# Block two with tokens on the partitions where the residual is added: 512-column weight streams instead of 256-column token streams

## The reference, cut to what matters

```
def hybrid_layer(x, ...):
    h = rmsnorm(x, norm_mix)             # x * rsqrt(mean(x*x) + 1e-6) * gain, per token
    z = h @ w_in                         # 1024 -> 4360 columns
    ... attention and mLSTM on z, two branch products, gates -> mixed
    x = x + mixed @ w_out                # 1024 x 1024
    u = jax.nn.relu(rmsnorm(x, norm_ffn) @ w_ff1)     # 1024 x 4096
    return x + (u * u) @ w_ff2           # 4096 x 1024
```

## Time and profile before

| | us |
|---|---|
| median of 3 runs | 2544.05 |
| lowest, highest | 2542.25, 2546.1 |
| the profiled execution's own time | 2542.61 |
| its span, first to last instruction | 2540.5 |

### The profile page before, as it was taken

How to read it: one execution, slowest core, us unless ns; L and a number is a source line. 1 busy time by engine, 2 the same in 40 slices (tenths; PEclk the granted TensorE clock), 3 DMA queues, 4 the chain that set the end, 5 groups by cost and what they waited for, 6 DMA issues and landing times.

```text
span 2540.5 us, 52442 instructions
## 1 busy us (share of the span) xinstructions
PE 2460.0 (97%) x20070; PEld 2318.3 (91%) x20086; DVE 1879.5 (74%) x2879; ACT 1278.6 (50%) x2103; POOL 1075.1 (42%) x620
## 2 busy tenths in 40 slices
PE   6999999999999999999999999999999999999999
PEld 4998999887989989989998788999889999989999
DVE  5875999678686787769997776775856677756676
ACT  3444456456554454444554565544654444654444
POOL 2434987412033233369872110333650344750344
PEclk9999999899999999999999999999999999999999
DMA  9885764333477568767643235875434466434564
GB/s 367 294 287 183 262 219 140 111 108 105 145 262 267 190 244 285 257 224 244 202 129 107 92 102 183 288 256 174 140 118 142 159 194 193 150 118 148 161 195 133
DMA packets 131496, 481.35 MB, mean 189 GB/s; under 512 B 14848, under 2 KB 14848, under 8 KB 130560
## 3 DMA queue, kind: packets, MB, share of 16 engines
q1 hardware_dynamic: 106992, 388.49, 45.8%
q0 software_dynamic: 23040, 83.90, 9.2%
q10 hardware_dynamic: 1296, 6.64, 0.7%
HBM read 475.82 MB, written 3.15 MB: 189 GB/s over the span
## 4 chain that ended last, share of the span: by engine, by line
PE 80%; DVE 9%; ACT 3%; POOL 3%; DVEq 2%; issue 1%; DMA 1%; ACTq 0%; SPq 0%; POOLq 0%
PE ps L473 23%; PE ps L474 22%; PE ps L475 22%; PE ps L627 2%; DVE ps L1754 2%; POOL eb L2147 1%; POOL ring_parts L2093 1%; ACT high L1143 1%; PE ps L1016 1%; PE ps L1005 1%; PE ps L484 1%; DVEq L1764 1%; DMA z<-ada_dram 1%; PE ps L487 1%; PE ps L485 1%
## 5 line engine op out<-in xcount | busy, mean ns | idle before, releaser
L474 PE MATMUL ps<-u_parts,high 128*128 128x256 f32 x3808 | 1061.8, 279 | 0.0
L474 PEld LDWEIGHTS ps<-u_parts,high 128*128 128x128 f32 x3808 | 720.2, 189 | 0.4
L1143 ACT ACTIVATE high<-ring 128x1024 fp32r<-128x1024 f32 x493 | 518.9, 1057 | 364.0 <-PE ps L475 329.4
L473 PE MATMUL ps<-ac_parts,high 128*128 128x256 f32 x1952 | 541.4, 277 | 9.9 <-DVE ring_parts L1541 9.4
L475 PE MATMUL ps<-ac_parts,ring_parts 128*128 128x256 f32 x1952 | 539.8, 277 | 0.0
L2098 POOL TENSOR_TENSOR ring_parts<-ring,high 128x1024 fp32r<-128x1024 f32 x88 | 223.5, 2539 | 407.9 <-ACT high L1143 407.8
L473 PE MATMUL ps<-h_parts,high 128*128 128x256 f32 x1328 | 380.6, 287 | 9.1 <-POOL ring_parts L2093 5.6
L473 PEld LDWEIGHTS ps<-ac_parts,high 128*128 128x128 f32 x1952 | 366.8, 188 | 12.5 <-DVE ring_parts L1541 11.6
L475 PE MATMUL ps<-h_parts,ring_parts 128*128 128x256 f32 x1328 | 373.5, 281 | 0.0
L2093 POOL TENSOR_TENSOR ring_parts<-ring,high 128x1024 fp32r<-128x1024 f32 x138 | 331.9, 2415 | 93.1 <-ACT high L1143 91.7
L475 PEld LDWEIGHTS ps<-ac_parts,ring_parts 128*128 128x128 f32 x1952 | 366.8, 188 | 0.0
(11 more groups left out here) (496 smaller groups left out, 5048.2 us busy)
## 6 DMA issues: line engine op xcount, KB each, us to landing
ring<-stream_dram SPq DMA_DIRECT2D x736, 512.0 KB, 3.6
xc<-ada_dram POOLq DMA_DIRECT2D x84, 512.0 KB, 5.9
z<-ada_dram POOLq DMA_DIRECT2D x36, 512.0 KB, 7.2
qr<-ada_dram POOLq DMA_DIRECT2D x36, 512.0 KB, 7.5
h_aside<-ac ACTq DMA_DIRECT2D x2, 1024.0 KB, 3.9
eb<-ada_dram POOLq DMA_DIRECT2D x4, 512.0 KB, 5.6
h<-h_aside ACTq DMA_DIRECT2D x2, 1024.0 KB, 7.0
conb<-con_dram ACTq DMA_DIRECT2D x1, 1032.0 KB, 8.7
```

Of the source, the lines that this page charges most:

```text
L473: mm(out, hi, xh, start=start, stop=False, **kw)
L474: mm(out, hi, xl, start=False, stop=False, **kw)
L1143: act(high_of(m, i), chunk_of(m, i), ACT.Copy).then_inc(made, 1)
```

## The change

In block two the residual has tokens on the partitions from W_out on: `m.ht[a]` is token half a, 128 tokens of 1024 features.

- W_out is packed by rows, like W_ff2. Each chunk of either is used by `token_product`: the stationary operand is the activation tile (128 features by 128 tokens, high or low part), and 512 columns of the weight chunk stream past it into one PSUM bank. Per chunk that is 2 token halves x 2 column halves x 3 = 12 matmuls of 512 columns, in the order of the four banks, where there were 24 of 256.
- DVE adds the banks to `m.ht` (`token_sums`) as each is complete.
- The norm's mean of squares is a row sum: one ACT pass over 1024 columns per token half that also adds up the row, then a root of one column (`token_roots`). DVE makes the reciprocal and a diagonal matrix of it (`token_scale`). TensorE multiplies the token tiles by this diagonal in f32, which scales and turns them to feature-major at once (`turn_tokens`). ACT makes the high parts and DVE the low parts straight from PSUM, with the gain (`token_highs`, `token_lows`).
- The norm at the start of layer 0 stays as it was. While layer 0's projections run, `turn_features` turns `m.h` once into `m.ht` by transposes (8 for each token half), and ACT copies them (`keep_features`).
- The output is stored token-major.

```diff
+def token_product(mm, m, i, xh, xl, start, ends=None):
+    hi, lo = high_of(m, i), low_of(m, i)
+    for a in range(2):
+        h, x = xh[:, a * P:(a + 1) * P], xl[:, a * P:(a + 1) * P]
+        def part(half, left, right, first, stop):
+            w = right[:, half * 512:(half + 1) * 512]
+            return mm(m.ps[:, 2 * a + half, :], left, w, start=first, stop=stop, skip_group_check=True)
+        for half in range(2):
+            part(half, h, hi, start, False)
+            part(half, h, lo, False, False)
+            last = part(half, x, hi, False, ends is not None)
+            if ends is not None and (a, half) != (1, 1):
+                last.then_inc(ends, 1)
+    return last
+FFN_BANKS = (6, 7, 0, 1)
+MIX_BANKS = (5, 6, 0, 1)
+def turned_tile(m, banks, k):
+    return m.ps[:, banks[k % 4], (k // 4) * S:(k // 4 + 1) * S]
...
 (tensor2)
+        def turn_tokens(s, banks, zeros):
+            products_of_zeros(mm, m, zeros)
+            def tile(a, k):
+                return mm(turned_tile(m, banks, k)[:, a * P:(a + 1) * P], m.ht[a][:, k * P:(k + 1) * P], m.diag[a],
+                          start=True, stop=True)
+            t.wait_ge(sem["scale"], 2 * s + 1)
+            for k in (0, 4, 1, 5, 2, 6):
+                tile(0, k)
+            t.wait_ge(sem["scale"], 2 * s + 2)
+            for k in range(4):
+                if k == 2:
+                    tile(0, 3)
+                    tile(0, 7)
+                tile(1, k)
+                tile(1, k + 4).then_inc(sem["turned"], 1)
+            products_of_zeros(mm, m, 2, 3)
+        def turn_features(a):
...
+            for k in range(ND):
+                last = nc.tensor.transpose(ps[:, 2 + k // 4, (k % 4) * P:(k % 4 + 1) * P], m.h[:, k, a * P:(a + 1) * P], con("ident"))
+            last.then_inc(sem["hturn"], 1)
-        rms(0)
+        if l == 0:
+            rms(0)
+        else:
+            turn_tokens(1, MIX_BANKS, 6)
...
         j = pair(E_IF + 1, j)
+        if l == 0:
+            turn_features(0)
...
         j = pair(E_QM, j)
+        if l == 0:
+            turn_features(1)
...
-        for q in range(4):
-            t.wait_ge(sem["outm"], at("outm", 5 + q))
...
-            if q == 0:
-                for tiles in (range(4), range(4, 6), range(6, ND)):
...
-        rms(1)
-        t.wait_ge(sem["usd"], at("usd", 2))
-        for b in range(4):
-            mm(ps[:, b, :], m.zero[:, 0:P], m.zero[:], start=True, stop=False, skip_group_check=True)
+        for k in range(ND):
+            if k % 2 == 0:
+                t.wait_ge(sem["ulo"], at("ulo", 12 + k // 2 + 1))
+            t.wait_ge(sem["lo"], at("lo", 8 + k + 1))
+            token_product(mm, m, E_OUT + k, m.uhi_ffn[:, k], m.ulo[:, k], k == 0, sem["sums"] if k == ND - 1 else None)\
+                .then_inc(done, 1)
+        turn_tokens(2 * l, FFN_BANKS, 6)
...
-        def down(i, f, fk, last=False):
+        def down(i, f, fk, start=False, last=False):
             t.wait_ge(sem["lo_g"], at("lo_g", MIX2 + fk + 1))
             t.wait_ge(sem["hidlo"], at("hidlo", fk + 1))
-            for n in range(ND):
-                x = product3(mm, ps[:, n // 2, (n % 2) * S:(n % 2 + 1) * S], m, i, n, m.hidhi[place2(f)],
-                             m.hidlo[place2(f)], start=False, stop=last, skip_group_check=True)
...
+            token_product(mm, m, i, m.hidhi[place2(f)], m.hidlo[place2(f)], start, sem["sums"] if last else None)\
+                .then_inc(done, 1)
...
 (scalar2)
+        def token_roots(s):
+            for k in range(2):
+                a.wait_ge(sem["xres"], 4 * s + 2 * k + 2)
+                act(m.junk, m.ht[k], ACT.Square, accum_out=m.squares_of[:, k:k + 1])
+                a.drain()
+                act(m.root_of[:, k:k + 1], m.squares_of[:, k:k + 1], ACT.Sqrt, scale=1.0 / D, bias=con("eps2", 1))\
+                    .then_inc(sem["root"], 1)
+        def token_highs(s, k0, banks, gain, dst, middle):
+            for n in range(ND):
+                if n < 4:
+                    a.wait_ge(sem["turned"], 4 * s + n + 1)
+                else:
+                    a.wait_ge(sem["ulo"], at("ulo", k0 + n - 3))
+                act(dst[:, n], turned_tile(m, banks, n), ACT.Identity, scale=par(gain, n)).then_inc(sem["uhi"], 1)
+                if n == 3:
+                    later_high(middle)
...
 (vector2)
+        def token_sums(s, factor, chunk):
+            for q in range(4):
...
+                if q < 3:
+                    v.wait_ge(sem["sums"], 3 * s + q + 1)
+                else:
+                    v.wait_ge(done, done_at(chunk))
+                part = m.ht[q // 2][:, (q % 2) * 512:(q % 2 + 1) * 512]
...
+        def token_scale(s, a):
+            v.wait_ge(sem["root"], 2 * s + a + 1)
+            nc.vector.reciprocal(m.scale_of[:, a:a + 1], m.root_of[:, a:a + 1])
+            v.drain()
+            ts(m.diag[a], con("ident"), m.scale_of[:, a:a + 1], None, ALU.mult).then_inc(sem["scale"], 1)
+        def token_lows(k0, banks, gain, uhi):
+            for n in range(ND):
+                v.wait_ge(sem["uhi"], at("uhi", k0 + n + 1))
+                stt(m.ulo[:, n], turned_tile(m, banks, n), par(gain, n), uhi[:, n], ALU.mult, ALU.subtract)\
+                    .then_inc(sem["ulo"], 1)
...
+        for i in range(E_OUT + 3, E_OUT + 8):
+            low_out(i)
+        low(E_FFN, 1)
+        token_sums(2 * l, 0.5, E_OUT + 7)
+        token_scale(2 * l, 0)
+        low(E_FFN + 1, 2)
+        token_scale(2 * l, 1)
+        token_lows(16, FFN_BANKS, "nffn", m.uhi_ffn)
...
 (pack2)
-        parts.append(by_column_tile(i["w_out"][l]))
+        parts.append(by_row_tile(i["w_out"][l]))
```

142 lines of the change are left out of this document (64 added, 78 removed).

## The result

The changed kernel takes 2544.37 us (median of 22 runs, 2538.91 to 2549.95) beside 2540.51 us for the kernel before (22 runs): ratio 1.0021, 95% interval 1.0013 to 1.0029. The forecast was 2528.8 and a gain of 15.2; measured is a loss of 3.9. (The three runs from which the forecast took its scale, 2544.05, are among the 22 and lay high.) The profiled execution took 2543.24 us, span 2541.6.

What follows compares the result with a forecast made beforehand. Bound by 256-column products' weight loads at full clock, plus norm waits at the seams. Products -11.8, seams after W_out -2.6, seam between layers -2.8, layer 0's turn +2.0: -15.2 us, giving 2528.8 us, range 2523 to 2536.

Steps and rivals of the forecast that it cites:

- The price of a 512-column f32r product: W_out and W_ff2 chunks: 0.216 us a product, taken from the 512-column bf16 row, so 2.592 us a chunk.
- The bound from above: Highest price considered for a 512-column f32r product in W_out and W_ff2: 0.228 us, twice 0.1142.
- at full clock the 256-column products ... are bound by their weight loads: Block two's products: loads, not the 0.1067 us of columns, set the 0.1142 us spacing, by some 0.0075 us each.
- next to no fixed extra shows: 256-column products at half clock: spacing 0.22 us against 0.2133 of pure columns, so there the columns bind.
- The first rival: W_out and W_ff2: f32r columns bind at 0.228 us per 512, chunks gain nothing; -3.4 us, 2540.6, chance 0.09.
- W_ff1 ... keep their form: W_ff1, the mixer and block one are unchanged in form; no time was charged for them.
- The clock: Mixer: one half-clock stretch more or less moves the forecast by 1.6 us.
- The seams: TensorE's waits for a norm shrink: two after W_out, -2.6 us together; one between the layers, -2.8 us.
- the pair's pace: First pair of chunks behind each seam: 48 products take 5.5 us instead of 5.8, a gain of 0.3.
- The turn of layer 0: Layer 0's projections: 2 x 8 transposes turn h to token-major, 1.0 us each time, +2.0 us.
- The feed: W_out and W_ff2: other engines keep up with the faster chunks; nothing charged, W_out's 0.6 us wait left as it is.
- the -11.8: W_out and W_ff2 products: 80 chunks each 0.148 us shorter, -11.8 us.

Runs made afterwards that it cites:

- E3: Changed kernel with each 512-column product of W_out and W_ff2 made as two of 256, the same activation tile loaded twice: 2544.78 us, ratio 1.0028.
- E1: Changed kernel with product bursts added behind its end, other engines idle: f32r 512 columns 0.229, 256 0.118, 128 0.112 us apart; bf16 512 0.216, 256 0.109.
- E9: Changed kernel with fifteen patterns of 256- and 512-column products behind its end, other engines idle: uncut steps, entered as they come, took 5.59 us.
- E10: Changed kernel with nineteen other patterns behind its end, other engines idle: uncut steps entered through one step with its first 512-column product cut took 5.47 us.
- E13: Changed kernel with idle-machine bursts behind its end, tile or stream moved by 16 columns between bursts: 512 columns 0.2267 to 0.2336 us apart, 256 columns 0.1133 to 0.1200.
- E16: Changed kernel with only the fourth place of block two's hidden tiles moved by 48 columns, to the other three's offset: 2537.97 us, ratio 1.0000.
- E6: Changed kernel with nine bf16 products of zeros in the wait before the first W_ff2 chunk: 2542.86 us, ratio 1.0013.
- E5: The changed kernel itself, run again unchanged: 2542.95 us, ratio 1.0022.
- E8: E6 with the first 512-column product of each chunk cut into two of 256: 2537.76 us, ratio 0.9993.
- E17: E16 with nine products of zeros in the hidden-tile wait and without the two products of zeros ending each turn: 2533.74 us, ratio 0.9976.
- E14: Changed kernel with real-role steps behind its end, other engines idle, loaded tile at its present offset or 16 columns on, seven cuts: uncut 5.49 and 5.55 us.

## Why the prediction was wrong

**The price of a 512-column f32r product** is the step that failed: "the nearest row is the 512-column one ... I take 0.216". That row is bf16. The bound from above, "twice 0.1142, if the pace belonged to the columns after all", was the right reading: 0.2267 at best, 0.2305 on average here. What led there was "at full clock the 256-column products ... are bound by their weight loads". E3 answers it: with the loads back the time is the same (2544.78). The 60-column rows do show a load at 0.110, and E1 has it at 0.112; but 256 f32r columns cost 0.1133 to 0.118 by themselves, and limits that lie 1 to 5% apart look like one in a single spacing. Half clock, where "next to no fixed extra shows", was taken for full clock too; but the extra shows only at full clock (0.427 for 512 f32r columns at half clock, which is the columns alone at 1.2 GHz). The first rival ("The columns bind", 2540.6, chance 0.09) had the price right. Its time was still a gain of 3.4 where a loss of 3.9 was measured: it lacked the next two points as well.

The Trainium skill ("TensorE: Matmul & The Clock Gate", Back-to-back issue gap) gives N / 2.4 + 2.5 ns as the gap of isolated products at full clock: 109.2 and 215.8. E1's bf16 rows agree (0.109 and 0.216); its f32r rows do not. I noted that the row of 0.1142 disagrees by 5 ns, and gave the 5 ns to the load.

**"W_ff1 ... keep their form"** was charged nothing. In 57 of 60 steps its 24 products each lost 3.6 ns against the mean of before, 0.086 us a step or about 5 us. The row of before (0.1142) was taken for the price of the product; E9, E10, E13 and E16 show that the same product has two paces, by the addresses and by what ran before it. By turning W_ff2 round, the change made the hidden tiles into loaded tiles, one of them at an odd offset. The first chunk with that tile put the steps on the slow pace, and in the changed kernel nothing brought them back.

**The clock.** I counted stretches at half clock only in the mixer. Two more appeared, behind the unchanged 2.44 us waits, 1.6 us each; in E6's trace they are gone. In the mixer one went: the kernel before has a granted clock of 0.50 from 2314.9 to 2318.3, the changed one has no such stretch between 2256 and 2364: about 1.6 us less in layer 1, the one stretch more or less that the range allowed for. Why the kernel before showed none behind the same waits stays open. It is hardly chance: the mean granted clock of all executions is 0.9902 before (33, beside E5 to E8) and 0.9888 for the change (22).

**The seams** were right in mechanism and nearly in size: -1.25 twice (forecast -1.0), -2.78 (-2.45). The further 0.3 each from the pair's pace did not come (from first to last start 5.68 us before, 5.72 after): the pair ran at 0.118, not 0.114. In E6, where it is the same, it ran at 0.113 in layer 0 (5.52), so this too was the pace and not the feed.

**The turn of layer 0** took 0.80 us twice (2.0 forecast in all). **The feed** was right: no wait in the steps; in W_out one of 0.5 us for a low part in layer 0, none in layer 1.

So, in the profiled executions: -5.3 from the seams, +1.6 from the turns, +3.2 and -1.6 from the clock, +6.6 from the steps, -0.6 in W_out (23.20 and 22.22 us before, 22.75 and 22.09 after). That is +3.9 of the +6.0. The other 2 lie in the mixers, whose products did not change; there more of them ran at the slow pace (520 and 475 spacings in the two layers, 390 and 384 before), which is about 1 us; the rest was not traced. Of the -11.8 only these -0.6 came.

What stays open: by which mechanism the addresses of tile and stream set the pace, what chooses the pace on entry, and whether f32r columns cost more than bf16 ones by their type or by the zeros in the bf16 rows. The Trainium skill ("SBUF — State Buffer", A bandwidth-pool intuition that's wrong) gives TensorE a second, independent read port for weight loads. By that alone the tile's address should not matter to the stream; E13 has it matter by up to 2.8%.

## What to carry to other kernels

Two limits that lie 1 to 3% apart (here a load of 0.110 to 0.112 and 256 f32r columns of 0.113) can't be told from one spacing: vary the columns with the load fixed, in the data type of the kernel, before giving the gain of a removed load. And look at the single spacings behind a mean. When operands change roles, look at the addresses of the new loaded tile and the new stream modulo 256 bytes; one tile out of four, moved by 192 bytes, was worth 0.2% here. A wait ahead of a long stretch of products can be worth filling when the clock falls behind it: 1.6 us each by the traces here, too little to show in the medians.

## What the runs showed of the hardware that I had not expected

512 f32r columns stood 0.2267 to 0.2336 apart and 256 columns 0.1133 to 0.1200, by the offsets of tile and stream (E13). With the offsets fixed, 256-column products have two paces, 0.1133 and 0.118, that each keep themselves up for 26 steps and more (E16, E17), with no other engine at work too (E9, E10). Block one of the kernel before, untouched by all this, shows both as well: mostly 0.1133 from 60 to 180 us and 0.1178 from 300 to 420 us. It is part of why runs of one kernel spread by 0.5%. In the profiles of the change, E1, E5, E9, E10, E13 and E14 block one is the same, yet of its 11000 spacings of 256 columns 1749 to 3196 are slow ones, and block two starts between 1781.19 and 1791.02 us. With the kernel before as an eighth the two go together (correlation 0.88, 4.7 ns for each slow spacing, where the paces differ by 4.5). What sets the pace from one execution to the next is not shown.
